# The dense weights stored as one array of 1 MB units, one 8 KB run per partition

## The reference

```python
def first_block(x, ...):
    for layer in range(2):
        if layer == 1:
            shared = nsa_shared_kv(h, kv_norm, kv_w, cmp_pe_k, cmp_w1_k, ...)
        mixed = retention_mixer(...) if layer == 0 else nsa_mixer(...)
        h = h + rms_norm(mixed, mix_norm_post[layer])
        h = h + rms_norm(swiglu_ffn(rms_norm(h, ...), ffn_w_in[layer], ffn_w_out[layer]), ...)

def second_block(x, c, ctx, ...):
    mod = silu(c) @ w_ada + b_ada
    proj = h @ w_in                      # 1024 x 5632
    merged = g_a * (y_a @ w_proj_a) + g_b * (y_b @ w_proj_b)
    x = x + g1 * (merged @ w_out)
    x = x + g2 * expert_choice_ffn(h2, w_router, w_exp_gate, w_exp_up, w_exp_down)
    return rmsnorm(x, final_g)
```

## Time and profile before

| | |
|---|---|
| runs | 2032.55, 2033.05, 2036.91 us |
| profiled execution: span | 2033.3 us |
| TensorE busy | 1618.4 us (80%) |
| VectorE, ScalarE, GpSimd busy | 753.3, 558.4, 133.2 us |
| DMA | 155,161 packets, 604.29 MB, 297 GB/s over the span |
| SP's queue (q1) | 146,224 packets, 587.23 MB |
| ScalarE's queue (q10), GpSimd's (q0) | 7,704 and 1,136 packets |

### The profile page before, as it was taken

How to read it: one execution, slowest core, us unless ns; L and a number is a source line. 1 busy time by engine, 2 the same in 40 slices (tenths; PEclk the granted TensorE clock), 3 DMA queues, 4 the chain that set the end, 5 groups by cost and what they waited for, 6 DMA issues and landing times.

```text
span 2033.3 us, 26312 instructions
## 1 busy us (share of the span) xinstructions
PE 1618.4 (80%) x11401; PEld 1112.2 (55%) x11401; DVE 753.3 (37%) x1082; ACT 558.4 (27%) x876; POOL 133.2 (7%) x111
## 2 busy tenths in 40 slices
PE   7999999999889999999998766556556566655555
PEld 7899999988568999897897311111111111111111
DVE  6766766675337755667755100000000000000000
ACT  4454544345545344445664000000000000000000
POOL 1001100000311300001300000000000000000000
PEclk9999899999889999999999887887877777878777
DMA  9845597648164655363267999999999999999997
GB/s 354 311 152 173 124 295 274 219 153 248 63 212 150 203 181 185 105 187 123 84 254 279 401 428 428 427 428 428 428 428 428 427 427 428 427 429 428 427 428 314
DMA packets 155161, 604.29 MB, mean 297 GB/s; under 512 B 6670, under 2 KB 107207, under 8 KB 127255
## 3 DMA queue, kind: packets, MB, share of 16 engines
q1 hardware_dynamic: 146224, 587.23, 73.5%
q10 hardware_dynamic: 7704, 11.24, 1.9%
q0 software_dynamic: 1136, 4.40, 1.7%
HBM read 595.51 MB, written 4.20 MB: 295 GB/s over the span
## 4 chain that ended last, share of the span: by engine, by line
PE 54%; DMA 34%; DVE 5%; another core or an unknown queue 3%; ACT 2%; issue 1%; POOL 0%; DVEq 0%; ACTq 0%
PE ps L748 19%; PE ps L817 11%; DMA dense_ring<-in_w_exp_gate 7%; DMA arena<-in_w_exp_down 5%; PE ps L1427 5%; DMA late_expert_slots<-in_w_exp_down 4%; PE ps L802 3%; DMA dense_tables<-in_w_exp_gate 2%; DMA dense_ring<-in_w_exp_down 2%; DMA arena<-in_w_exp_gate 2%; DMA residual_normed_squares<-in_w_exp_up 2%; DMA late_expert_slots<-in_w_exp_gate 2%; DMA late_expert_slots<-in_w_exp_up 2%; DMA residual_normed_squares<-in_w_exp_gate 2%; DMA dense_ring<-in_w_exp_up 2%
## 5 line engine op out<-in xcount | busy, mean ns | idle before, releaser
L650 DVE TENSOR_TENSOR split_operands<-dense_ring,split_operands 128x1024 fp32r<-128x1024 f32 x282 | 343.0, 1258 | 201.3 <-ACT split_operands L642 201.0
L748 PE MATMUL ps<-split_operands 128*128 128x256 f32 x3360 | 412.5, 284 | 2.2 <-issue 1.2
L748 PEld LDWEIGHTS ps<-split_operands 128*128 128x128 f32 x3360 | 406.7, 192 | 4.4 <-issue 2.6
L642 ACT ACTIVATE split_operands<-dense_ring 128x1024 fp32r<-128x1024 f32 x290 | 290.5, 1050 | 313.5 <-PE ps L748 152.4
L2601 DVE TENSOR_TENSOR arena<-arena,ps 128x512 f32<-128x512 f32 x16 | 11.0, 688 | 567.0 <-PE ps L1427 567.0
L1908 ACT ACTIVATE arena<-ps 128x512 f32<-128x512 f32 x16 | 9.6, 597 | 583.3 <-PE ps L1427 583.3
L817 PE MATMUL ps<-split_operands 128*128 128x256 f32 x1248 | 154.0, 286 | 2.7 <-DVE split_operands L660 2.7
L817 PEld LDWEIGHTS ps<-split_operands 128*128 128x128 f32 x1248 | 152.5, 194 | 4.2 <-DVE split_operands L660 3.5
L817 PE MATMUL ps<-hidden_split,split_operands 128*128 128x256 f32 x960 | 118.6, 283 | 0.8 <-DVE split_operands L650 0.8
L817 PEld LDWEIGHTS ps<-hidden_split,split_operands 128*128 128x128 f32 x960 | 116.6, 192 | 1.0 <-DVE split_operands L650 1.0
L2609 DVE TENSOR_TENSOR tabs<-ps,tabs 128x512 f32<-128x512 f32 x16 | 11.1, 692 | 271.5 <-PE ps L1456 271.5
(11 more groups left out here) (369 smaller groups left out, 1822.4 us busy)
## 6 DMA issues: line engine op xcount, KB each, us to landing
dense_ring<-in_ffn_w_in SPq DMA_DIRECT2D x44, 1024.0 KB, 5.1
late_expert_slots<-in_w_exp_up SPq DMA_DIRECT2D x22, 2048.0 KB, 50.1
dense_ring<-in_w_exp_gate SPq DMA_DIRECT2D x21, 2048.0 KB, 50.1
arena<-in_w_exp_gate SPq DMA_DIRECT2D x20, 2048.0 KB, 49.6
arena<-in_w_exp_down SPq DMA_DIRECT2D x20, 2048.0 KB, 50.2
dense_ring<-in_w_exp_up SPq DMA_DIRECT2D x17, 2048.0 KB, 49.5
late_expert_slots<-in_w_exp_down SPq DMA_DIRECT2D x16, 2048.0 KB, 50.0
arena<-in_w_exp_up SPq DMA_DIRECT2D x14, 2048.0 KB, 50.7
```

Of the source, the lines that this page charges most:

```text
L642: act.activation(w_hi[:, n % 2, c], ring[U % RING][:, c], ACT.Copy).then_inc(hi_ready, 1)
L650: dve.tensor_tensor(w_lo[:, n % 2, c], ring[U % RING][:, c], w_hi[:, n % 2, c], ALU.subtract).then_inc(lo_ready, 1)
L748: mm = pe.matmul(ps[:, bank, b * T:b * T + T], left, right, start=k == 0 and i == 0, stop=k == 7 and i == 2)
```

## The change

The 150 dense units that are not parts of `w_ada_2` are laid out ahead of the launch in one array, `dense`, of shape (150, 128, 2048), in the order of use. Within a unit each partition's 8 KB are contiguous. All loads take `dense[n]`; the kinds of source and of slot views go. SP issues the same transfers into the same slots behind the same waits, in the same order; no instruction of another engine changes. The two halves of the first unit become 4 KB runs. In the loop of the second network the register picks the unit.

```diff
+DENSE_NO = {U: i for i, U in enumerate(U for U in range(U_END) if U not in range(U_ADA, U_NO))}
...
-        def col_src(w, n0):
-            return w.rearrange("(k p) n -> p k n", p=P)[:, :, n0:n0 + 256] if isinstance(n0, int) else \
-                w.rearrange("(k p) n -> p k n", p=P)[:, :, bass.ds(n0, 256)]
-        def row_src(w, u):
-            v = w.rearrange("(c p) n -> p c n", p=P)
-            return v[:, 2 * u:2 * u + 2, :] if isinstance(u, int) else v[:, bass.ds(u * 2, 2), :]
+        def dense_src(U):
+            if U in range(U_ADA, U_NO):
+                return ada_v[:, U - U_ADA, 0:UNIT]
+            return a["dense"][DENSE_NO[U]]
...
-            def load(U, src, k, round_=0):
-                dst = {8: slot8, 4: slot4, 2: slot2}[k](U) if k else ring[U % RING]
+            def load(U, src=None, round_=0):
...
-                sp.dma_start(dst, src).then_inc(landed[U % RING], 16)
+                sp.dma_start(ring[U % RING], dense_src(U) if src is None else src).then_inc(landed[U % RING], 16)
-            first = col_src(w_in, 256 * order[0])
+            first = dense_src(U_RET).rearrange("p (k n) -> p k n", k=8)
...
-                        for c in range(2):
-                            gu(U0 + 5 + 3 * c, i * 2 + (2 + c), i)
-                            load(U0 + 7 + 3 * c, row_src(w2, i * 2 + (1 + c)), 2, i)
+                        for U in range(U0 + 5, U0 + 11):
+                            unit = a["dense"][bass.ds(i * 6 + DENSE_NO[U], 1)]
+                            load(U, unit.rearrange("u p n -> p (u n)"), i)
...
+    def cols_of(w, n0):
+        return in_rows(w[:, n0:n0 + 256])
+    def rows_of(w, u):
+        return in_rows(w[256 * u:256 * u + 256])
+    def half_of(w, n0, half):
+        return in_rows(w[512 * half:512 * half + 512, n0:n0 + 512])
...
+    def dense_units():
+        w = x["ret_w_in"][0]
+        units = [cols_of(w, 256 * c) for hd in range(4) for c in (hd, 4 + hd)]
+        units += [half_of(w, 2 * D + 512 * (u // 2), u % 2) for u in range(8)]
...
+        return np.stack(units)
```

More of the change, by code:

```diff
@@ L440, in program @@
         block = ctx.enter_context(nc.Block())
-        def col_src(w, n0):
-            return w.rearrange("(k p) n -> p k n", p=P)[:, :, n0:n0 + 256] if isinstance(n0, int) else \
-                w.rearrange("(k p) n -> p k n", p=P)[:, :, bass.ds(n0, 256)]
-        def row_src(w, u):
-            v = w.rearrange("(c p) n -> p c n", p=P)
-            return v[:, 2 * u:2 * u + 2, :] if isinstance(u, int) else v[:, bass.ds(u * 2, 2), :]
+        ada_v = a["w_ada_2"].rearrange("(k p) n -> p k n", p=P)
+        def dense_src(U):
+            if U in range(U_ADA, U_NO):
+                return ada_v[:, U - U_ADA, 0:UNIT]
+            return a["dense"][DENSE_NO[U]]
         def slot8(U):
             return ring[U % RING].rearrange("p (k n) -> p k n", k=8)
[L455 to L463, removed]
         by_pair = [ring_mem[:, U % RING // 2, :] for U in (U_PB + 2, U_WO, U_WO + 2)]
@@ L537, in _ @@
             for u in range(1, 24):
[L538 to L541, removed]
+                load(U_RET + u)
                 if u in after:
@@ L544, in _ @@
             for u in range(8):
-                load(U_RO + u, row_src(a["ret_w_out"], u), 2)
+                load(U_RO + u)
             def ffn(f, U0):
[L548 to L556, removed]
+                for U in range(U0, U0 + 5):
+                    load(U)
@@ L574, in _ @@
+                load(U0 + 32)
             ffn(0, U_F0)
[L575 to L583, removed]
@@ L584, in _ @@
-            for u in range(4):
-                load(U_NO + u, row_src(a["nsa_w_out"], u), 2)
-            ffn(1, U_F1)
[L587 to L592, removed]
+            for U in range(U_KV, U_F1):
+                load(U)
@@ L593, in _ @@
+            ffn(1, U_F1)
+            for U in range(U_IN2, U_PA):
+                load(U)
+            for U0 in (U_PA, U_PB, U_WO):
                 for u in range(4):
-                    load(U0 + u, row_src(a[w], u), 2)
+                    load(U0 + u)
                 if U0 == U_PB:
@@ L2758, in in_rows, with ffn_units, gate_and_up @@
         return w.reshape(-1, P, w.shape[1]).transpose(1, 0, 2).reshape(P, -1)
+    def cols_of(w, n0):
[4 more added lines that the diff above has]
+        return in_rows(w[512 * half:512 * half + 512, n0:n0 + 512])
+    def ffn_units(w1, w2):
+        def gate_and_up(j):
+            return [cols_of(w1, 256 * j), cols_of(w1, HID + 256 * j)]
+        units = gate_and_up(0) + gate_and_up(1) + [rows_of(w2, 0)]
+        for j in range(2, PAIRS):
+            units += gate_and_up(j) + [rows_of(w2, j - 1)]
+        return units + [rows_of(w2, PAIRS - 1)]
+    def dense_units():
+        w = x["ret_w_in"][0]
+        units = [cols_of(w, 256 * c) for hd in range(4) for c in (hd, 4 + hd)]
+        units += [half_of(w, 2 * D + 512 * (u // 2), u % 2) for u in range(8)]
+        units += [cols_of(w, 256 * c) for c in range(16, 24)]
+        units += [rows_of(x["ret_w_out"][0], u) for u in range(8)]
+        units += ffn_units(x["ffn_w_in"][0], x["ffn_w_out"][0])
+        units += [cols_of(x["kv_w"], 256 * c) for c in (0, 1, 2, 4, 3, 5)]
+        units += [in_rows(x[n][D * u:D * u + D]) for u in range(2) for n in ("cmp_w1_k", "cmp_w1_v")]
+        units += [cols_of(x["nsa_w_in"][0], 256 * u) for u in range(4)]
+        units += [rows_of(x["nsa_w_out"][0], u) for u in range(4)]
+        units += ffn_units(x["ffn_w_in"][1], x["ffn_w_out"][1])
+        units += [half_of(x["w_in_2"][0], D + 512 * (u // 2), u % 2) for u in range(4)]
+        units += [cols_of(x["w_in_2"][0], 256 * c) for c in IN2_ORDER[4:]]
+        for n in ("w_proj_a_2", "w_proj_b_2", "w_out_2"):
+            units += [rows_of(x[n][0], u) for u in range(4)]
+        assert len(units) == len(DENSE_NO)
+        return np.stack(units)
     def pairs(pe):
```

25 lines of the change are left out of this document (9 added, 16 removed).

## The result

| | before | after |
|---|---|---|
| runs | 11 | 11 |
| median us | 2035.59 | 2040.68 |
| lowest and highest | 2032.55 to 2039.07 | 2034.01 to 2044.28 |
| span of the profiled execution | 2033.3 | 2036.5 |
| TensorE busy | 1618.4 (80%) | 1604.4 (79%) |

The ratio is 1.0024, with a 95% interval of 1.0014 to 1.0033: by its middle 4.9 us slower, which is over the fifth of a per cent (4.1 us) that the prediction took as its bound of no change, and the median lies above its range. Eight more runs of before put its median 2.5 us above the three that the prediction started from. A run's time is also some 1.8 us above the span of the same execution (2038.29 to 2036.5 us for after), so the profile of before showed a usual execution, near 2035.1 us, and not one just above the median of the three runs, as I had taken it.

The account below looks back on a forecast made before the run. TensorE's chain was taken to bound the kernel up to 1134.10 us, then expert transfers, leaving dense transfers off the path. Terms of 0.3 and 1.0 us made 1.3 us on 2033.05, about 2034.3 us, range 2030.3 to 2038.0.

Parts of the forecast that it names:

- Packets and rate: All DMA: packets fall from 155,161 to about 62,400; a lone dense unit lands in 4.8 us, not 5.1.
- Its cover: Dense stage: the ring of six units, about 5.8 us each, hides up to about 75 us of saved DMA time.
- Unit 2, term 0: Near 20 us: ScalarE's 0.78 us wait for unit 2 goes, but VectorE's work is what is late; worth 0.
- (a): Head of the chain, 4 to 5 us: `cols` meets SP's longer packets; 0.3 us slower, between 0 and 0.46.
- (b): Start: `tabs` and `rel_bias` land at about 21.2 us, past 1.5 us of slack; 1.0 us slower, between 0 and 2.6.
- R4: Rival at the start: `tabs` lands within its slack, the neighbour effect is absorbed; 2033.3 us, chance 0.27.
- (c): Shifted keys, 452 to 469 us: 2 us earlier to 3 us later, inside 4.4 us of slack; worth 0.
- R1: Slower rival: shifted keys 7.5 us later, TensorE waits 3.1 us at L2202; 2037.5 us, chance 0.14.
- R2: Faster rival: DMA saving shows at TensorE's gap, 2031.8 us, or 2027 us with fewer low-clock stretches; chance 0.10.
- (d): Near 270 us: SP gains against `bias_skew`, which ends some us later; TensorE does not wait; worth 0.
- (e): Experts, from 1134 us: same runs, slots and waits; the stream only moves with TensorE's work before it.
- R3: Rival: 8 KB runs still go out in short packets, count well above 62,400; 2033.05 us, chance 0.04.

Follow-up runs that it names:

- both_short: The changed kernel with old short runs in the first eight units and the six beside the shifted keys, 14 of 150; ratio to before 1.0002.
- keys_short: The changed kernel with old short runs only in the six units that travel beside the shifted keys; ratio to before 1.0013.
- bias_later: The changed kernel with ScalarE's bias table load moved from ahead of the eight shifted key copies to behind them; ratio to before 1.0052.
- all_short: The changed kernel's single array, but every unit in the run lengths of before; ratio to before 1.0003.
- fix_start_bias: The changed kernel with the bias table load moved behind the shifted keys and old short runs in the first eight units; ratio to before 1.0019.
- before_pause: The kernel before plus one unused VectorE reciprocal lengthening TensorE's gap ahead of unit 2, no transfer changed; ratio to before 1.0006.
- only_keys_long: The single array with old runs everywhere except 8 KB runs in the six units beside the shifted keys; ratio to before 1.0014.
- start_short: The changed kernel with old short runs in the first eight units alone; ratio to before 1.0017.
- keys_4k: The changed kernel with old short runs in the first eight units and 4 KB runs in the six beside the shifted keys; ratio to before 1.0022.
- bias_last: The changed kernel with old short runs in the first eight units and the bias table load moved behind the doubled keys; ratio to before 1.0014.

## Why the prediction was wrong

**The base.** Of the 6.4 us between 2034.3 and 2040.68 us, 2.5 are the base: the three runs had a median of 2033.05 us, eleven have 2035.59. The span of the profile (2033.3 us) did not lie 0.25 us above a usual time but 1.8 us below its own run's. The rest is the 1.3 us that were forecast against the 5.1 measured.

**What bounds the kernel: right.** The experts' rate is unchanged and 136 long-run units change nothing (both_short).

**Packets and rate: right**, 62,361 packets, 4.9 us a unit, 430 GB/s, and no packet of SP's cut at 4 KB. Its cover held: worth 0.

**Unit 2, term 0: right as far as it can be read.** VectorE's row is what is late there.

**(a) `cols`, 0.3 us: right mechanism, size 0.69 us.** Over the kernels it takes 4.74 to 5.05 us with the start in old runs and 5.45 to 5.74 in new ones, so the upper end of 0.46 us was passed. With the first unit alone in old runs it takes 5.11 us, half of the way back. I had counted only the 4.4 turns per engine of the one microsecond from 4 to 5 us; that the turns before it make up the rest is argued, not shown.

**(b) `tabs` and `rel_bias`, 1.0 us: right, 0.84 us**, the growth of TensorE's gap. `rel_bias` landed 2.7 us later after its issue, where I had worked out 2.6 (less the slack of 1.5 that makes 1.1, not the 1.0 that I took). The turns are one for one with long packets too; DMA of after, 15 to 16 us:

```profile
q10 hardware_dynamic: 20, 0.22, 51.5%
q1 hardware_dynamic: 26, 0.19, 44.6%
```

The Trainium skill (DMA: Bandwidth & Descriptors, Queues, rings and completion order) says that an engine goes round the queues that have work and changes only between packets; these rows and the earlier trace rows agree. What I missed here is 1.5 us of unit 2 at the lower clock: 3.1 us are lost up to the row of 240, and not 1.3. Neither part is there in every profile: keys_short and bias_later have the long start too, but their first 48 matmuls took 8.57 and 8.00 us instead of 7.42, the transfers were down in time behind these, and the gap is 1.20 us in both, as in before. So R4, the late transfer absorbed, holds in some.

**(c) The shifted keys, 0: wrong, and this is the step that failed**, in three ways.

First the slack. I wrote that L1012 needs the first two of the four pieces of L2202, ready at 470.95 us, and had 4.4 us. The code has TensorE wait for all four (`pe.wait_ge(blocks_set, 4)`, L1005). The fourth ends at 469.10 + 3.71 = 472.81 us, so the slack was 2.5 us.

Second the lateness. I bounded it at 3 us by the bytes that SP's queue could move ahead, and held against my first rival that it counts bytes twice. Measured against the issue of the keys it is 10.35 - 5.97 = 4.4 us. It is one copy that is so late. The eight shifted keys, from issue to landing, of before and of after:

```profile
DMA to landing us min/median/max: 8.4/9.6/11.5
```

```profile
DMA to landing us min/median/max: 9.2/11.3/15.7
```

The middle grows by 1.7 us, the slowest, which is the last one issued, by 4.2. The slowest takes 15.6 to 16.1 us in all five kernels whose runs beside the keys are of 4 or 8 KB, and 11.7 to 12.6 in all_short, keys_short and both_short. A count of bytes or turns that treats the eight alike, as mine did, cannot give that, and why it is the last one is open.

The DMA views show what passed from about 3 us before the keys' issue to their landing, of before (450 to 469 us) and of after (453 to 476):

```profile
DMA packets 5855, 5.81 MB, mean 306 GB/s; under 512 B 195, under 2 KB 5854, under 8 KB 5854
...
q10 hardware_dynamic: 3253, 3.17, 58.5%
q1 hardware_dynamic: 2601, 2.62, 51.5%
```

```profile
DMA packets 4288, 7.32 MB, mean 318 GB/s; under 512 B 263, under 2 KB 3843, under 8 KB 3843
...
q10 hardware_dynamic: 3779, 3.66, 60.9%
q1 hardware_dynamic: 508, 3.64, 45.3%
```

The window of after is 4 us longer, so that more passed in it says nothing; whose bytes they are does. SP's queue moved 1.0 MB more before the keys were down, a whole unit, and ScalarE's 0.5 MB more. SP issues as before, each unit 3.1 us later like the rest. The last of the four, from issue to landing, issued at 462.3 us in before and at 465.5 in after:

```profile
DMA to landing us min/median/max: 15.8/15.8/15.8
```

```profile
DMA to landing us min/median/max: 10.8/10.8/10.8
```

In before it lands at 478.1 us, 9 us behind the last key; in after at 476.3, 0.3 us ahead of it: 508 packets of SP's against 3779 of ScalarE's take half of the bytes of the window. My "no more than what is queued" was the right kind of bound, but it has to take in units that are issued while the short packets are still waiting.

Third the price of the wait. 4.4 us of lateness less 2.5 of slack is 1.9 us, and 1.5 to 2.1 is what TensorE waits in the five kernels that have this wait. But the 64 matmuls behind it take 8.8 to 9.3 us in them instead of 7.12, since TensorE's granted clock is 0.50 for 3.4 to 6.8 us. That is the same again, so the event costs about 3.7 us in the profile of after. Neither (c) nor R1 has a price for the clock; I had only said, under R2, that it can add to R1's side. The lower clock stands beside every such wait (in bias_later and fix_start_bias too, beside TensorE's 3.2 or 3.1 us for ScalarE); of the seven profiles without one, five have none and two, all_short and before_pause, have 3.4 us of it beside a wait of 0.2 us. That the wait brings it is not shown: in after it began 0.9 us ahead of the wait, at about 477.9 us, and in only_keys_long about 0.8 us ahead. What TensorE did ahead of that place is the same in every kernel: 32 matmuls of 48 columns (L968 of after), 3.67 us.

**(d) and (e), 0: right as far as it can be read.** The experts' stage took 2.0 us longer in after's profile, and as much in that of before_pause. The sign that I gave, the experts' first transfer on the chain at about 1135.4 us, came out at 1135.30 by luck: 7.2 us were lost up to the keys' matmuls, and 5.9 of them came back.

**The rivals.** R1, the keys late with TensorE waiting at L2202, is the place and the wait that happened, at 2037.5 us and a chance of 0.14. Its 4.4 us over before stand against the measured 4.9, and that is luck: it took 7.5 us of lateness (measured 4.4), 4.4 of slack (2.5), a start of 1.3 (3.1) and nothing for the clock. What it lacks in absolute time is mostly the base, since the three runs shown lay 2.5 us under the median of eleven. It stood low because of the misread slack and the argument of the double count. R2's remark that a change of waits shifts the clock's stretches either way is right in the profile, but both_short and all_short show no gain from it. R3 is out by the packet count, R4 by VectorE's wait of 0.89 us in after's profile, though not in all.

**How far it is shown.** By the ratios: the length of the runs is the cause (all_short), it acts in 14 units (both_short), and the keys' six alone carry about 0.0014 of 0.0024 (only_keys_long; start_short, which leaves them long, has 0.0017). The start's share, 0.0013 in keys_short, is a second part of the same size by its middle value. The intervals of the two overlap and do not give a split. That it works by turns on the DMA engines rests on the landings and the packet rows, and the length of a turn alone does not give the size (keys_4k). Not settled: why the clock falls behind the gap of 1.7 or 2.05 us ahead of unit 2 and not behind the 2.8 us of before_pause; how much of a late start is given back before 640 us (in only_keys_long five of the twelve runs lie under before's median of 2035.38 us, at 2034.02 to 2035.19, and one at 2045.63); why the last key alone is so late; and why bias_last, without any wait at either place, has no ratio of 1.

## What to carry to other kernels

Longer runs on one DMA queue were not free for the others here: where two queues took turns packet by packet, the one with the small packets fell behind, even though the other moved its bytes faster. Before lengthening the runs of a stream that is not late, look for each small transfer of another queue that has a reader with little slack, and read that slack from the count that the reader's semaphore waits for, not from the first use. Where a long row of small packets is moved within its own queue to cure it, look at the next thing behind it on the issuing engine: in bias_later that was late instead.

## What the runs showed of the hardware

A run of 8 KB or 16 KB went out as one packet (62,361 packets in after; 27 packets for 0.44 MB) and took one turn of its engine (26 of SP's beside 20 of ScalarE's from 15 to 16 us). The kernel with runs of 4 KB beside the keys was nearly as late as those with 8 KB (VectorE's wait 10.0 us, and 10.2 to 10.7; with 1 KB 6.0 to 7.0).

Issuing got slow too: the eight doubled keys took ScalarE 6.25 and 5.69 us to issue in before and after, and 10.8 and 10.7 us in bias_later and fix_start_bias, with the bias table's load right ahead of them and the shifted keys ahead of that. The load alone did not do it: in before and after it stands right ahead of the eight shifted keys, which took 5.4 and 5.5 us to issue.

The granted clock was 0.50 for 3.4 or 6.8 us beside TensorE waits of 1.5 to 3.2 us near 480 us, twice from 0.8 to 0.9 us ahead of the wait, and in two profiles for 3.4 us beside a wait of 0.2 us; it was 0.50 for some 3.4 us in the unit behind gaps of 1.7 and 2.05 us at 26 us; yet it stayed at 1.00 behind a gap of 2.8 us at 28 us.
